# The first expert's rows gathered tile by tile around the last router, in place of twelve identity turns

## The reference

```python
h = _layernorm(DEEPNORM_ALPHA * h + mix, ln1_g[i], ln1_b[i])

logits = (jnp.einsum('ld,de->le', h, w_router) + b_router).astype(jnp.float32)
top_val, top_idx = lax.top_k(logits, TOP_K)
gates = jax.nn.softmax(top_val, axis=-1).astype(h.dtype)
flat_e = top_idx.reshape(-1)
order = jnp.argsort(flat_e)
tok = order // TOP_K
group_sizes = jnp.bincount(flat_e, length=N_EXPERTS).astype(jnp.int32)
xs = h[tok]
hgu = lax.ragged_dot(xs, w_gate_up, group_sizes) + b_gate_up[e_sorted]
act = _clamped_swiglu(hgu)
out = lax.ragged_dot(act, w_down, group_sizes) + b_down[e_sorted]
out = out * gates.reshape(-1)[order][:, None]
```

## Time and profile before

| | |
|---|---|
| median of 3 runs | 2251.17 us (2249.81 to 2257.55) |
| the profiled execution | 2253.48 us |
| its span on the core | 2251.7 us |
| TensorE busy | 2206.9 us (98%) |
| VectorE busy | 1687.7 us (75%) |
| ScalarE busy | 1243.1 us (55%) |
| GpSimd busy | 568.7 us (25%) |
| chain that ended last | TensorE 84%, VectorE 8%, GpSimd 4%, ScalarE 1% |

### The profile page before, as it was taken

How to read it: one execution, slowest core, us unless ns; L and a number is a source line. 1 busy time by engine, 2 the same in 40 slices (tenths; PEclk the granted TensorE clock), 3 DMA queues, 4 the chain that set the end, 5 groups by cost and what they waited for, 6 DMA issues and landing times.

```text
span 2251.7 us, 29477 instructions
## 1 busy us (share of the span) xinstructions
PE 2206.9 (98%) x10718; PEld 1811.7 (80%) x10718; DVE 1687.7 (75%) x1616; ACT 1243.1 (55%) x1285; POOL 568.7 (25%) x399
## 2 busy tenths in 40 slices
PE   8999999999999999999999999989999999999998
PEld 6778878888888888888888888877777878888886
DVE  7577699998999999999999999982567446423334
ACT  5246267776787777877768777742444522422320
POOL 4170169982232322322223222200220010000000
PEclk9999999999999999999999999999999999999999
DMA  5230279999999999999999999943221332323221
GB/s 194 67 124 25 87 279 390 398 387 376 391 382 400 378 391 386 381 400 376 393 384 384 397 379 389 362 159 111 60 80 38 120 123 94 112 76 111 99 88 38
DMA packets 142081, 552.29 MB, mean 245 GB/s; under 512 B 11712, under 2 KB 12864, under 8 KB 124976
## 3 DMA queue, kind: packets, MB, share of 16 engines
q1 hardware_dynamic: 128928, 507.95, 58.4%
q0 software_dynamic: 10592, 38.41, 6.6%
q10 hardware_dynamic: 2480, 4.80, 0.6%
HBM read 522.66 MB, written 25.69 MB: 244 GB/s over the span
## 4 chain that ended last, share of the span: by engine, by line
PE 84%; DVE 8%; POOL 4%; ACT 1%; issue 1%; DMA 1%; DVEq 0%; SPq 0%; POOLq 0%; ACTq 0%
PE PS L428 79%; DVE low L2319 3%; PE PS L811 1%; PE PS L760 1%; ACT act L1981 1%; POOL act L3019 1%; POOL xs L3003 1%; DVE st L2071 1%; DMA ring<-w_down 1%; DVE small L2691 1%; POOL xs L2998 1%; PE PS L637 0%; DMA acc_d<-act,to_c 0%; DVE act L2103 0%; DVE ring_parts L2596 0%
## 5 line engine op out<-in xcount | busy, mean ns | idle before, releaser
L428 PE MATMUL PS<-act_parts 128*128 128x512 f32 (+2 forms) x3392 | 1052.9, 398 | 2.1 <-DVE xs L2475 1.5
L2319 DVE TENSOR_TENSOR low<-ring,act_parts 128x2048 fp32r<-128x2048 f32 x380 | 859.9, 2316 | 32.6 <-ACT act_parts L1719 32.5
L428 PEld LDWEIGHTS PS<-act_parts 128*128 128x128 f32 (+2 forms) x3392 | 619.1, 188 | 143.0 <-issue 9.5
L1719 ACT ACTIVATE act_parts<-ring 128x2048 fp32r<-128x2048 f32 x384 | 706.8, 1911 | 12.0 <-PE PS L428 9.2
L428 PE MATMUL PS<-low,act_parts 128*128 128x512 f32 x1584 | 618.3, 390 | 0.0
L428 PE MATMUL PS<-act_parts,ring_parts 128*128 128x512 f32 (+3 forms) x1696 | 466.5, 374 | 0.0
L428 PEld LDWEIGHTS PS<-act_parts,ring_parts 128*128 128x128 f32 (+1 forms) x1696 | 302.3, 187 | 67.5 <-issue 13.3
L428 PEld LDWEIGHTS PS<-low,act_parts 128*128 128x128 f32 x1584 | 298.3, 188 | 58.8
L428 PE MATMUL PS<-ring_parts,act_parts 128*128 128x512 f32 (+2 forms) x1208 | 272.9, 383 | 3.1 <-DVE act_parts L2768 2.1
L428 PEld LDWEIGHTS PS<-ring_parts,act_parts 128*128 128x128 f32 (+1 forms) x1208 | 219.7, 188 | 50.2 <-issue 3.9
L428 PE MATMUL PS<-ring_parts 128*128 128x512 f32 (+1 forms) x672 | 250.8, 380 | 0.0
(11 more groups left out here) (305 smaller groups left out, 1905.6 us busy)
## 6 DMA issues: line engine op xcount, KB each, us to landing
ring<-w_gate_up SPq DMA_DIRECT2D x264, 1024.0 KB, 8.5
ring<-w_down SPq DMA_DIRECT2D x132, 1024.0 KB, 7.9
ring<-w_ff SPq DMA_DIRECT2D x16, 2048.0 KB, 7.7
ring<-w_in SPq DMA_DIRECT2D x12, 2048.0 KB, 9.8
ring<-w_o SPq DMA_DIRECT2D x1, 4096.0 KB, 14.6
ring<-w_out SPq DMA_DIRECT2D x2, 2048.0 KB, 7.8
acc_d<-ring POOLq DMA_DIRECT2D x5, 512.0 KB, 6.5
act<-x SPq DMA_DIRECT2D x4, 512.0 KB, 5.6
```

The costliest lines, as they stand in the source:

```text
L428: return eng.matmul(o, lhsT, rhs, start=first, stop=last, **kw)
L1719: A_(W1hi[c % CS], W1[c], ACT.Copy).then_inc(sem["high"], 1)
L2319: tt(W1lo[c], W1[c], W1hi[c % CS].bitcast(F32), ALU.subtract).then_inc(sem["low"], 1)
```

## The change

- TensorE: the twelve identity turns behind the turn of tile 3 leave; the 22 ahead of it stay. first_rows is no longer a half after the other but a tile after the other: `first_rows(t)` multiplies OH0 of tile t with both halves of H1[:, t, :], into banks 0 and 6. The order is now: turn of tile 3 (banks 1 and 2), rows of tile 0, ranks(1), router(3) (bank 7), ranks(2), rows of tile 1, ranks(3), rows of tile 2, rows of tile 3. Before, both halves used banks 0 and 1.
- VectorE: first_hot(0) moves ahead of routed_tile(1), right behind the norm of tile 3. The copy of the turned half of tile 3 leaves.
- ScalarE: it copies both turned halves of tile 3, the second ahead of the DMA that writes the tile to memory. `router(3)` waits for the fifth h1T_act signal in place of the fourth h1T_dve.

```diff
--- before.py
+++ after.py
@@ -72,9 +72,9 @@
     "probs_psum": [("pT_psum", 32), ("pTa_psum", 32), ("pTb_psum", 16)],
     "heads_psum": [("o_ready", 32), ("oa_psum", 32), ("ob_psum", 16)],
     "sums_psum": [("ss_psum", 11), ("logits_psum", 4), ("y_psum", 2), ("sum_psum", 8), ("gate0_psum", 8)],
-    "turned_act": [("hT_act", 4), ("oT_hi", 8), ("h1T_act", 4), ("y_hi", 2), ("x2T_hi", 8), ("o2T_hi", 8), ("m_hi", 8), ("x3T_hi", 8),
+    "turned_act": [("hT_act", 4), ("oT_hi", 8), ("h1T_act", 5), ("y_hi", 2), ("x2T_hi", 8), ("o2T_hi", 8), ("m_hi", 8), ("x3T_hi", 8),
                    ("ff_hi", 32)],
-    "turned_dve": [("hT_dve", 5), ("h1T_dve", 4), ("x2T_lo", 8), ("m_lo", 8), ("x3T_lo", 8), ("ff_lo", 32)],
+    "turned_dve": [("hT_dve", 5), ("h1T_dve", 3), ("x2T_lo", 8), ("m_lo", 8), ("x3T_lo", 8), ("ff_lo", 32)],
     "copied_act": [("z_raw", 14), ("vg_raw", 5), ("qr_raw", 4), ("qn_out", 4), ("v_out", 5), ("va2_out", 4),
                    ("qa2_out", 4), ("ka2_out", 4), ("qb2_out", 4), ("kb2_out", 4), ("vb2_out", 4)],
     "exp_act": [("prob", 32), ("proba", 32), ("expb", 32)],
@@ -675,7 +675,7 @@
                 eng.wait_ge(*past("ln1_out", t + 1))
                 for hf in range(2):
                     turn([H1[:, t, (4 * hf + j) * P:(4 * hf + j + 1) * P] for j in range(4)], "h1T_psum",
-                         (("h1T_act", "h1T_dve")[hf], t + 1))
+                         ("h1T_act", t + 1 + hf) if t == NT - 1 or not hf else ("h1T_dve", t + 1))
 
             def router(t):
                 eng.wait_ge(*past("router_in", 80))
@@ -685,7 +685,7 @@
                 free[b] = past("tile_routed", 3 * t + 1)
                 for k in range(KD):
                     if k == KD // 2:
-                        eng.wait_ge(*past("h1T_dve", t + 1))
+                        eng.wait_ge(*(past("h1T_act", NT + 1) if t == NT - 1 else past("h1T_dve", t + 1)))
                     ins = mm(PS[:, b, 0:E], H1T[:, k, t * P:(t + 1) * P], wr[:, k, :], k == 0, k == KD - 1)
                 ins.then_inc(put("logits_psum", b), 1)
 
@@ -737,23 +737,30 @@
                     eng.transpose(PS[:, 6, 0:P], ident, ident)
 
             ranks(0)
-            cur[0] = 0
+            cur[0] = 1
             turn_ident(22)
             turn_tile(NT - 1)
-            turn_ident(12)
+
+            ROW_BANKS = (0, 6)
+            for hf in range(2):
+                take(ROW_BANKS[hf], "rows_out", hf + 1)
+
+            def first_rows(t):
+                eng.wait_ge(*past("first_hot", 2 * t + 2))
+                for hf in range(2):
+                    ins = mm(PS[:, ROW_BANKS[hf], :], OH0[:, t, :], H1[:, t, hf * 512:(hf + 1) * 512], t == 0, t == NT - 1)
+                    if t == NT - 1:
+                        ins.then_inc(put("rows_psum", ROW_BANKS[hf]), 1)
+
+            first_rows(0)
             ranks(1)
+            cur[0] = 7
             router(NT - 1)
             ranks(2)
-
-            def first_rows(hf):
-                take(hf, "rows_out", hf + 1)
-                for t in range(NT):
-                    if hf == 0:
-                        eng.wait_ge(*past("first_hot", 2 * t + 2))
-                    ins = mm(PS[:, hf, :], OH0[:, t, :], H1[:, t, hf * 512:(hf + 1) * 512], t == 0, t == NT - 1)
-                    if hf == 0 and t == 0:
-                        ranks(3)
-                ins.then_inc(put("rows_psum", hf), 1)
+            first_rows(1)
+            ranks(3)
+            first_rows(2)
+            first_rows(3)
 
             def turn_rows():
                 for k in range(KD):
@@ -761,8 +768,6 @@
                                         xg.rearrange("s (p k) -> s k p", k=KD)[:, k, :], ident)
                 ins.then_inc(sem["rows_turned"], 1)
 
-            first_rows(0)
-            first_rows(1)
             take(3, "count_out", 1)
             for t in range(NT):
                 ins = mm(PS[0:E, 3, 0:1], Mm[:, t, :], ones[:, 0:1], t == 0, t == NT - 1)
@@ -1722,6 +1727,10 @@
                 eng.wait_ge(*past("h1T_psum", 2 * t + 1))
                 A_(H1T[:, 0:4, t * P:(t + 1) * P], four(bank_of("h1T_psum", 2 * t + 1)), ACT.Copy).then_inc(
                     signal("h1T_act"), 1)
+                if t == NT - 1:
+                    eng.wait_ge(*past("h1T_psum", 2 * t + 2))
+                    A_(H1T[:, 4:8, t * P:(t + 1) * P], four(bank_of("h1T_psum", 2 * t + 2)), ACT.Copy).then_inc(
+                        signal("h1T_act"), 1)
                 eng.wait_ge(*past("ln1_out", t + 1))
                 eng.dma_start(h1_d[t * P:(t + 1) * P, :], H1[:, t, :]).then_inc(signal(f"h1_{t}_out", 16), 16)
 
@@ -2350,6 +2359,14 @@
                 eng.tensor_reduce(Mm[:, t, :], OH[:, chosen, :].rearrange("p k e -> p e k"), AX.X, ALU.add).then_inc(
                     signal("tile_routed"), 1)
 
+            def first_hot(t):
+                eng.wait_ge(*past("rank_psum", t + 1))
+                eng.tensor_copy(R2[:, t, :], bank_of("rank_psum", t + 1)[:, 0:E]).then_inc(
+                    signal("first_hot"), 1)
+                eng.wait_ge(*latest("first_hot"))
+                ts(OH0[:, t, :], iotas, R2[:, t, 0:1], Mm[:, t, 0:1], ALU.is_equal, ALU.mult).then_inc(
+                    signal("first_hot"), 1)
+
             eng.wait_ge(*past("h0_scaled", NT))
             for t in range(NT):
                 projected(0, t)
@@ -2369,22 +2386,14 @@
                 eng.wait_ge(*past("mix", 8 + 2 * t + 2))
                 stats(HN, 1, t)
                 affine(HN, ln1G, ln1B, 1, t, to=H1)
+                if t == NT - 1:
+                    first_hot(0)
                 if t >= 2:
                     routed_tile(t - 2)
             def spread(x, n):
                 return x.rearrange("p (k o) -> p k o", o=1).to_broadcast([P, TOPK, n])
 
-            def first_hot(t):
-                eng.wait_ge(*past("rank_psum", t + 1))
-                eng.tensor_copy(R2[:, t, :], bank_of("rank_psum", t + 1)[:, 0:E]).then_inc(
-                    signal("first_hot"), 1)
-                eng.wait_ge(*latest("first_hot"))
-                ts(OH0[:, t, :], iotas, R2[:, t, 0:1], Mm[:, t, 0:1], ALU.is_equal, ALU.mult).then_inc(
-                    signal("first_hot"), 1)
-
-            turned_tile(NT - 1)
             routed_tile(NT - 2)
-            first_hot(0)
             first_hot(1)
             routed_tile(NT - 1)
             first_hot(2)
```

## The result

| | before | after |
|---|---|---|
| median, side by side, 22 runs each | 2251.48 us (2249.81 to 2257.55) | 2256.02 us (2251.38 to 2260.77) |
| ratio | | 1.0017, 95% interval 1.0011 to 1.0024 |
| profiled execution | 2253.48 us, span 2251.7 | 2260.45 us, span 2258.6 |
| chain that ended last | TensorE 84%, VectorE 8% | TensorE 82%, VectorE 10% |

In this set of runs the changed kernel is slower by 4.5 us by the medians (0.20%), 0.17% by the ratio. That is less than the 0.3% that the prediction called measurable; 22 runs on each side resolve it.

The account below looks back on a forecast made before the run. TensorE bounds the expert loop, which the change leaves alone. Turns -1.39, rounding and overlap +0.11, ScalarE's rows copies +0.35 give -0.93 at turn_rows; -0.6 was taken at the end: 2251.17 - 0.6 = 2250.6 us, range 2246.5 to 2256.

Parts of the forecast that it names:

- the 0.3%: Whole kernel: smallest difference a measurement can tell from no change, 6.8 us; staying the same was given 0.93.
- The stage: Tile 3's norm to first weight product: no added TensorE wait, count products 1.28 us earlier, turn_rows 0.93 us earlier.
- lists late by 1.3 us: VectorE: the last first_hot starts at 288.45, not 287.12, pushing gates, one-hot lists and bias halves by 1.3 us.
- The margin at rows_low(0): Ahead of the first expert: rows_low(0) ends at 297.4, just ahead of TensorE at 297.49, only 0.1 us margin.
- the gap ahead of turn_rows: TensorE's one hole in the changed stage, between count products and turn_rows: 0.8 us, 0.44 before.
- -0.35 if VectorE carries, -0.93 if GpSimd does, I take the middle, -0.6: Behind the first expert: how much of the 0.93 us lead reaches the end; -0.35 to -0.93 given 0.50.
- the third rival: GpSimd loses its place against VectorE's lows: slower, 2252.6 us (one miss) to 2254.9 (two); chance 0.19.
- one miss costs one low, +1.4: GpSimd operation started behind a VectorE low: 2.3 us less the 0.93 lead; two misses +3.7.
- The clock rival: TensorE loses its clock in the changed stage: about 1.7 us lost, +0.8 net, 2252.0 us; chance 0.05.
- a cap on the gain: Near 409 us: if the whole gain passes, VectorE's readiness caps it at 1.75 us, 2249.4 us; chance 0.14.
- The range: Measured time between 2246.5 and 2256 us, about 3 us below the lowest and 1 us above the highest case.
- the slowest case by the text: GpSimd misses its place twice behind VectorE's lows: +3.7 us, 2254.9 us.

Follow-up runs that it names:

- the two later sets: Changed kernel, unaltered, timed twice more beside the kernel before, 11 runs each: 2253.12 us (ratio 1.0011) and 2251.63 us (ratio 1.0004).
- taking one of them away: Changed kernel with GpSimd's count tables moved behind its select copies, which removed TensorE's second wait near 329 us: 2255.80 us, ratio 1.0017.
- the control with the early addition: Kernel before with GpSimd's first addition of a product issued ahead of the first table of overfull experts: 2252.66 us, ratio 0.9999.
- The four added operations: Kernel before with four more GpSimd operations in front of its first table, and so of its first addition: 2263.09 us by five of six runs, ratio 1.0049.

## Why the prediction was wrong

*The stage.* Right to 0.2 us, and to 0.1 from turn_rows on: the count products at 13.03 us behind the zero (13.24 by the sum), turn_rows at 14.37 (14.44), the first weight product at 18.83 (18.90). Rows copies back to back, lists late by 1.3 us, no wait of TensorE: all as worked out. The margin at rows_low(0), feared at 0.1 us, was enough. The clock was at 1.00 up to there, and the gap ahead of turn_rows (0.93 us) brought no fall.

*The lead behind it.* The step "-0.35 if VectorE carries, -0.93 if GpSimd does, I take the middle, -0.6" holds in the executions without a blocked GpSimd: at item 3 three traces of the changed kernel read 147.70 to 147.79 against 148.41 and 148.45, thus -0.6 to -0.75. It is real, and where the addition is not late it is kept: at item 9 the same three read 373.4 to 374.3 against 374.5 and 375.1. It is lost, with more, in the trace in which the addition is late.

*What failed is the third rival, by its price and by its chance.* Its mechanism came: GpSimd's copy of the first tokens lasted 6.27 us and not 1.86, the select copies 2.57 and not 0.53, the issue of the addition 3.7 and not 1.7, in the same trace. The same copy lasted as long as one low of VectorE in most traces (1.86 us) and ended with the third low in two (6.27 us). The Trainium skill ("SBUF — State Buffer", section "SBUF: two separate sides") has the exclusive lock that fits these lumps; that the lock is their cause was not tested. But "one miss costs one low, +1.4" left out what stands behind a late addition: TensorE's wait, already 1.5 us long, grows (to 3.1 to 4.6 us at the weight load in the three traces with a long issue), and then the clock falls for 3.4 or 6.8 us. In the first trace of the changed kernel the loss from item 3 to item 9 is 231.44 - 226.06 = 5.4 us: 2.8 of wait (4.55 against 1.71) and the rest, 2.5, which fits products at the lower level. Added to the 0.6 us by which it is late at item 3 already, it is 6.0 us behind before at item 9. The sum had one miss at +1.4 and two at +3.7.

*The clock rival had the right mechanism in the wrong place.* I looked for a gap in the changed stage only, and found one of 0.8 us; it was 0.93 and harmless. The rows for the right place were in my hands: the earlier trace rows had TensorE waiting 1.5 us behind the same addition, and the earlier trace rows what the clock does after a gap of 2.85 us. I used the first as a cap on the gain and never asked what it would do if it grew. By the Trainium skill ("TensorE: Matmul & The Clock Gate", section "HAM oscillation — how this bites in real kernels") idle gaps bring the clock down; the traces agree for the waits of 2.5 us and more, but the two falls near 285 us came without such a gap.

*The range* ended at 2256.0 and the median of 22 runs was 2256.02. It had 1 us above the slowest case by the text, and no case that joined the two mechanisms. The change stayed within the 0.3%, to which the prediction gave 0.93. In the two later sets the median (2253.12 and 2251.63) lies inside the range; so how far the first set went is in part the draw of that set.

*What stays open.* Whether, and why, the addition is late more often in the changed kernel. Its issue lasts 3.0 to 3.7 us in three traces, which have the waits of 3.1 to 4.6; of the four traces of the unaltered changed kernel only the first is among them. In the other traces with the addition in its old place it lasts 1.7 us. The sets of the same program differ by 5 us between them, so the phase of GpSimd against VectorE cannot be the work of this change alone. The clock's share is known only by the estimate from the table, about 1 us for each 3.4 us low. And the part behind item 9, which varies by 4 us with falls of its own, was never held still; how much of the 4.5 us lies there is not known, since one slow execution of the first set was traced and none near its median.

## What to carry to other kernels

A microsecond gained in front of a stretch that is paced by another engine need not vanish quietly. It can lengthen the wait that is already there, and a wait of TensorE of 1.5 us that grew to 2.5 or more cost the clock behind it as well. So before a lead is counted, look at the next waits of TensorE and at what would happen if each grew by a few microseconds. Here the wait went away by a change of order on GpSimd: the addition that others wait for ahead of a table that nobody yet needs (22 runs, none above 2253.61 us). For differences of 0.2%, one trace for each kernel misleads, and so does one set of runs: two places in the first trace looked alike, taking one of them away brought no gain, and three sets of the same pair gave +4.5, +1.4 and -0.4 us.

## What the runs showed of the hardware

- The clock fell though TensorE had hardly paused. In the control with the early addition it was busy 9.60 of 10.00 us ahead of the fall, with identity turns, turns of a tile and 32-column products, and then ran at 0.50 for some 6.8 us. Filler turns thus do not always hold the clock. All falls near 285 us lie in kernels with the twelve turns (2 of 7 traces), none in those with 512-column products in their place (0 of 11); that is too few traces to call it a rule.
- The low stretches measured near 330 and 430 us were 3.4 or 6.8 us long, and the length did not go by the wait: one of 3.0 us near 328 us was followed by 3.4 us low in the first trace of before and by 6.8 us in the second. Near 430 us, waits of TensorE's weight load of up to 1.8 us brought none, one of 2.5 us did.
- Beside VectorE's lows (2.3 us each) operations of GpSimd vary in length: the same 128x1 copy took 0.19, 1.87 or 6.27 us, and the same issue of an indirect DMA 1.7 to 3.7 us. The four added operations took 17.07 us, where 2.4 were meant by the estimate of 0.6 each.
- In the stretch from item 3 to item 9, 3.4 us at half clock cost about 1 us and 6.8 us about 2, by an estimate from 16 traces with their waits taken off.
